# Where the gathered modulation rows and the context blocks stand in TensorE's queue: a two-model transformer stack on one core

## The reference, cut to what matters

```python
for l in range(2):
    ml, mc = silu(c) @ w_ada[l] + b_ada[l], silu(c_ctx) @ w_ada[l] + b_ada[l]   # 9 vectors of 1024 each
    lat += 0.5 * ml[2] * swiglu(rmsnorm(lat) * (1 + ml[1]) + ml[0])             # ffn1, both streams
    cx  += 0.5 * mc[2] * swiglu(rmsnorm(cx)  * (1 + mc[1]) + mc[0])
    lat, cx = mixer(modulated lat, modulated cx)                                # w_in: 1024 -> 3584, then w_out
    lat += 0.5 * ml[8] * swiglu(modulated lat)                                  # ffn2; cx too in layer 0
x = rmsnorm(lat) * g_final
for layer in range(2):                                                          # the second model, 256 tokens
    x += attention(rmsnorm(x) * g) ;  x += relu(rmsnorm(x) * g @ up) ** 2 @ down
```

## Time and profile before

| what | value |
|---|---|
| median of three runs | 2677.27 us |
| the profiled execution's own time | 2683.47 us |
| its span, first to last instruction | 2681.6 us |
| TensorE (PE) busy | 2593.1 us |
| VectorE, ScalarE, GpSimd busy | 1199.1, 1111.2, 885.9 us |
| mean granted TensorE clock | 0.985 of full |

### The profile page before, as it was taken

The page is one execution under the profiler, slowest core; times in us unless marked ns, Lnnn a source line. Parts: engine busy times, 40 slices in busy tenths (PEclk is TensorE's granted clock), DMA queues, the critical chain, the costliest instruction groups (busy, mean ns, idle before and its releaser), DMA issues.

```text
span 2681.6 us, 43982 instructions
## 1 busy us (share of the span) xinstructions
PE 2593.1 (97%) x17121; PEld 2306.9 (86%) x17121; DVE 1199.1 (45%) x1801; ACT 1111.2 (41%) x1544; POOL 885.9 (33%) x1092
## 2 busy tenths in 40 slices
PE   7999999999999999999999999888999999999999
PEld 5787778988888777787777888888999999998999
DVE  4222224227662222252232247654446666556744
ACT  4312333635334222243122247535574555446543
POOL 1222231320013223222232226304554445553554
PEclk9999999999999999999999999999999999999999
DMA  6343632430023333333334333323454434452444
GB/s 251 135 176 141 173 141 109 142 127 1 32 79 149 142 141 142 142 115 130 133 149 158 127 145 138 109 86 143 179 186 153 157 142 179 182 186 105 166 177 153
DMA packets 58527, 376.89 MB, mean 141 GB/s; under 512 B 6223, under 2 KB 12007, under 8 KB 14216
## 3 DMA queue, kind: packets, MB, share of 16 engines
q1 hardware_dynamic: 56988, 371.53, 37.4%
q10 hardware_dynamic: 1388, 3.16, 0.8%
HBM read 370.46 MB, written 3.16 MB: 139 GB/s over the span
## 4 chain that ended last, share of the span: by engine, by line
issue 54%; PE 26%; POOL 17%; DVE 1%; ACT 1%; POOLq 0%; DMA 0%; SPq 0%; DVEq 0%; ACTq 0%
POOL WL L1919 17%; PE PSA L566 8%; PE PSA L567 8%; PE PSA L568 8%; PE PSA L645 1%; ACT WH L1366 0%; POOLq L398 0%; PE PSA L1200 0%; PE PSA L1227 0%; PE PSA L1151 0%; PE PSA L1128 0%; PE PSA L1172 0%; DMA X<-in_x 0%; DMA RAW<-in_weights 0%; POOLq L1917 0%
## 5 line engine op out<-in xcount | busy, mean ns | idle before, releaser
L1919 POOL TENSOR_TENSOR WL<-RAW,WH 128x256 fp32r<-128x256 f32 x1088 | 885.7, 844 | 1783.3 <-ACT WH L1366 1783.3
L1366 ACT ACTIVATE WH<-RAW 128x1024 fp32r<-128x1024 f32 x544 | 545.7, 1050 | 923.8 <-PE PSA L568 879.0
L1942 DVE TENSOR_TENSOR WL<-RAW,WH 128x1024 fp32r<-128x1024 f32 x272 | 340.4, 1252 | 1113.0 <-ACT WH L1366 1112.8
L566 PE MATMUL PSA<-HH,WH 128*128 128x512 f32 (+1 forms) x1664 | 597.7, 359 | 22.1 <-DVE HL L2037 5.2
L567 PE MATMUL PSA<-HL,WH 128*128 128x512 f32 (+1 forms) x1664 | 590.3, 355 | 0.0
L568 PE MATMUL PSA<-HH,WL 128*128 128x512 f32 (+1 forms) x1664 | 589.4, 354 | 0.0
L566 PE MATMUL PSA<-GH,WH 128*128 128x256 f32 (+1 forms) x1664 | 528.1, 317 | 4.8 <-DVE GL L1959 4.8
L567 PE MATMUL PSA<-GL,WH 128*128 128x256 f32 (+1 forms) x1664 | 521.2, 313 | 0.0
L568 PE MATMUL PSA<-GH,WL 128*128 128x256 f32 (+1 forms) x1664 | 521.0, 313 | 0.0
L566 PEld LDWEIGHTS PSA<-HH,WH 128*128 128x128 f32 x1664 | 317.3, 191 | 81.6 <-issue 22.4
L568 PEld LDWEIGHTS PSA<-HH,WL 128*128 128x128 f32 x1664 | 317.4, 191 | 43.8
(11 more groups left out here) (326 smaller groups left out, 2968.8 us busy)
## 6 DMA issues: line engine op xcount, KB each, us to landing
RAW<-in_weights SPq DMA_DIRECT2D x272, 1024.0 KB, 4.9
ADA<-in_w_ada SPq DMA_DIRECT2D x65, 1024.0 KB, 4.9
Zada<-in_w_ada SPq DMA_DIRECT2D x7, 1024.0 KB, 15.6
scratch_bias<-BREL ACTq DMA_DIRECT2D x1, 2048.0 KB
SUMS<-in_c_sums SPq DMA_DIRECT2D x1, 1664.0 KB, 8.2
TB<-scratch_bias SPq DMA_DIRECT2D x1, 1536.0 KB, 12.1
X<-in_x SPq DMA_DIRECT2D x1, 1024.0 KB, 6.0
X<-in_ctx SPq DMA_DIRECT2D x1, 1024.0 KB, 9.0
```

What stands on the lines that cost most here:

```text
L566: pe.matmul(out, a_hi, b_hi, start=start, stop=False)
L1366: act.activation(WH[:, j, 4 * h:4 * h + 4, :], RAW[:, j, 4 * h:4 * h + 4, :], ACT.Copy)\
L1919: ins = pool.tensor_tensor(WL[:, j, kb, :], RAW[:, j, kb, :], WH[:, j, kb, :].bitcast(F32), ALU.subtract)
L1942: dve.tensor_tensor(WL[:, j, 0:4, :], RAW[:, j, 0:4, :], WH[:, j, 0:4, :].bitcast(F32), ALU.subtract)\
```

## The change

In words:

1. **Turns.** `ADAR` goes. In w_in the rows still gather in bank 7; in ffn_up and down phases they gather in half of bank 6. The turn no longer waits there for the modulations to be read (`mods_read`); the finish does. In ffn_up and down phases the turn moves from behind the pair's second slot to behind its first. The finish of the phase before now stands behind the next phase's first turn instead of ahead of it.
2. **Added sums.** `added_sums` for a late norm moves from the end of the down phase to behind the first slot of the next phase.
3. **Context blocks.** `pair_by_stream` works by block: slot 0 on context `kb` 0 to 4, then alternately slot 1 on `kb` 0, 1, 2 and slot 0 on `kb` 5, 6, 7, then the sums of squares, then slot 1 on `kb` 3 to 7, then the latent halves. The wait for the second pair of banks, and with it that for slot 1's low part, moves ahead of slot 0's `kb` 5. In w_in both token blocks are done for each `kb`; which bank holds which token block changes, and ScalarE's read-out with it.
4. **First norm.** Four buffers of 256 columns in place of two for the squares. `first_root(0)` stands one block later.

```diff
-        ADAR = PSA[:, 7, 256:512]
+        def ada_rows_of(ph):
+            return bank(7 if ph["kind"] == "w_in" else 6)[:, 256:512]
             def ada_turn(ph, it):
-                pe.wait_ge(mods_read, n.at(mods_read))
+                if ph["kind"] == "w_in":
+                    pe.wait_ge(mods_read, n.at(mods_read))
                 pe.wait_ge(ada_landed, it * 16 + 16 * (ph["ada"] // 2 - 6))
-                ada_rows(ADAR, ADA, it, it == 0, it == ada_its(ph) - 1)
-            def ada_finish(ph):
+                ada_rows(ada_rows_of(ph), ADA, it, it == 0, it == ada_its(ph) - 1)
+            def ada_finish(ph, gated=0):
                 its = ada_its(ph)
+                pe.wait_ge(mods_read, n.at(mods_read) - gated)
                 pe.wait_ge(rows_copied, ph["ada"] // 2 + its)
                 ada_columns(2 * (ph["ada"] % ADA_HELD), 0, its)
             def ada_behind(ph, it, j):
-                if j == 0 and it == 0 and ph["turns"]:
-                    ada_finish(ph["turns"])
-                if has_ada(ph, it):
-                    if j == (0 if ph["kind"] == "w_in" else 1):
-                        ada_turn(ph, it)
-                    elif ph["kind"] == "w_in" and it == ada_its(ph) - 1:
-                        ada_finish(ph)
+                if j == 0 and has_ada(ph, it):
+                    if it == 0 and ph["turns"]:
+                        pe.wait_ge(rows_copied, ph["ada"] // 2)
+                    ada_turn(ph, it)
+                    if it == 0 and ph["turns"]:
+                        ada_finish(ph["turns"], int(PLAN[PLAN.index(ph) - 1]["kind"] == "gate"))
+                if j == 1 and ph["kind"] == "w_in" and it == ada_its(ph) - 1:
+                    ada_finish(ph)
...
                         if (ph["squares"] or ph["feeds"]) and 2 * it + j:
                             if not adds_squares(ph):
                                 unit_sums(ph, 2 * it + j - 1)
-                            elif 2 * it + j == 3:
-                                added_sums(ph)
                         if begins and j == 0:
                             if ph["late"]["fed_by"].get("by_pair"):
                                 unit_sums(ph["late"]["fed_by"], 2)
+                            else:
+                                added_sums(ph["late"]["fed_by"])
                             unit_sums(ph["late"]["fed_by"], 3)
...
                 def pair_by_stream():
...
+                        for m in range(2):
+                            if kind == "w_in":
+                                tok = slice(P * (2 * s + m), P * (2 * s + m) + P)
+                                mm = three(bank(2 * j + m)[:, t], HH[:, kb, tok], HL[:, kb, tok], WH[:, j, kb, :], WL[:, j, kb, :],
+                                           kb == 0, kb == KB - 1)
...
-                    for j in range(2):
-                        pe.wait_ge(bank_read[j], ph["unit"] + BANK_CREDIT)
-                        half(j, 1)
-                        if j == 0:
-                            part_sums(3, 0)
-                    for j in range(2):
-                        half(j, 0).then_inc(mm_done, 1)
+                    ahead = 5
+                    pe.wait_ge(bank_read[0], ph["unit"] + BANK_CREDIT)
+                    for kb in range(KB):
+                        if kb == ahead:
+                            pe.wait_ge(bank_read[1], ph["unit"] + BANK_CREDIT)
+                        if kb >= ahead:
+                            block(1, 1, kb - ahead)
+                        block(0, 1, kb)
+                    part_sums(3, 0)
+                    for kb in range(KB - ahead, KB):
+                        block(1, 1, kb)
+                    for j in range(2):
+                        for kb in range(KB):
+                            mm = block(j, 0, kb)
+                        mm.then_inc(mm_done, 1)
...
             def first_norm():
...
+                quarters = S2[:].rearrange("p a (b t) -> p (a b) t", b=2)
+                for s in range(2):
+                    for kb in range(KB):
+                        n.take(sq_ready)
+                        pe.matmul(bank(4 - s)[:, 0:NL], ones, quarters[:, kb % 4, :], start=kb == 0, stop=kb == KB - 1)\
+                            .then_inc(sq_used, 1)
...
-                            out = Ztm[:, (which + 1) % 4, per * m:per * m + per, 256 * j:256 * j + 256]
+                            blocks = slice(m, 4, 2) if i < 2 else slice(per * m, per * m + per)
+                            out = Ztm[:, (which + 1) % 4, blocks, 256 * j:256 * j + 256]
...
-                dve.tensor_copy(ROWS[:, 0, :], ADAR).then_inc(rows_copied, its)
+                dve.tensor_copy(ROWS[:, 0, :], ada_rows_of(ph)).then_inc(rows_copied, its)
```

More of the change, by code:

```diff
@@ L783, in pair_by_stream, with block @@
                 def pair_by_stream():
[L785 to L789, removed]
-                            if j == 0:
[L791 to L803, removed]
+                    def block(j, s, kb):
+                        t = streams(512)[s][1]
+                        if s == 1:
+                            slot_half(ph["slot"] + j, kb)
+                        if j == 0:
+                            pe.wait_ge(h_ready, hbase + KB * (1 - s) + kb + 1)
+                        for m in range(2):
[3 more added lines that the diff above has]
+                                           kb == 0, kb == KB - 1)
+                            else:
                                 w = slice(P * m, P * m + P)
@@ L825, in body_of_two_slot_units @@
                             mm.then_inc(mm_done, 1)
-                        if ph["feeds"] and 2 * it + v == 3:
-                            added_sums(ph)
                 def units_by_half():
@@ L848, in units_by_half @@
                             mm.then_inc(mm_done, 1)
-                            if half and u == 3:
-                                added_sums(ph)
                 def units_by_pair():
@@ L1296, in first_norm @@
             def first_norm():
[L1298 to L1303, removed]
+                quarters = S2[:].rearrange("p a (b t) -> p (a b) t", b=2)
[4 more added lines that the diff above has]
+                            .then_inc(sq_used, 1)
+                        if s and kb == 3:
+                            first_rows(0)
+                n.squares += 2 * KB
                 first_rows(1)
@@ L1455, in norm @@
                     act.activation(RSTD[:, 0:1], PR[:, PRM["sel"]:PRM["sel"] + 1], ACT.Sqrt)
[L1456 to L1464, removed]
+                    quarters = S2[:].rearrange("p a (b t) -> p (a b) t", b=2)
+                    for s, t in streams(N):
+                        if s:
+                            act.wait_ge(ctx_landed, 16)
+                        for kb in range(KB):
+                            if s == 0 and kb % 4 == 0:
+                                n.take(x_ready)
+                            if n.squares >= 4:
+                                act.wait_ge(sq_used, n.squares - 3)
+                            act.activation(quarters[:, kb % 4, :], X[:, kb, t], ACT.Square).then_inc(sq_ready, 1)
+                            n.squares += 1
+                            if s and kb == 3:
+                                first_root(0)
                     first_copy(0)
```

## The result

The changed kernel takes 2658.39 us, the median of four runs (2657.78 to 2659.84). The kernel before, run beside it, took 2680.14 us (2676.43 to 2684.7, four runs). The ratio is 0.9908, 95% interval [0.9896, 0.992]: faster by 21.8 us. The profiled execution's span is 2656.0 us where it was 2681.6.

The account below looks back on a forecast made before the run. TensorE, busy 2593.1 of 2681.6 us, was taken as the bound, so only standstills and half clock could move. Terms 1.6 + 8.6 - 1.1 + 7.6 + 0.6 + 3.8 = 21.1 off 2677.3 gave 2656.2 us, range 2649 to 2669 with rivals.

Parts of the forecast that it names:

- A: First norm: four square buffers shorten the first sums, so the first weights start earlier; 1.6 us saved, at most 4.3.
- B: The two w_in behind a norm by stream: latent half done 5.3 us earlier each, less 2 for low clock; 8.6 saved.
- C: The two ffn_up behind a norm by stream: one wait exchanged for another, nothing gained; -1.1 us, between +2 and -5.
- D: Turn behind the first slot: SyncE issues loads a slot sooner, the 4.81 us standstill near 337 us goes; 7.6 saved.
- E: Finish behind the turn: costs nothing, and the one wait for a group goes; 0.6 us saved.
- F: Added sums later: the 1.9 us wait at 2021 us and the half clock behind it go; 3.8 us saved.
- The group is late instead: Under the bias table's DMA the group lands at 329.3 us whenever issued; D = -4.0, time 2668; chance 0.17.
- The standstills stay, low clock after each: Waiting for slot 1's low part lowers the clock at all four norms; B = 3, C = -5, time 2666; chance 0.2.
- Only small change: Both first rivals at once: about 0 to 8 us saved, 2669 to 2677 us; chance 0.08.
- slower: Turns wait on loads that collide with weights, say ten by 3 us; 8 us slower, 2685 us; chance 0.04.

Follow-up runs that it names:

- e2_blocks: The kernel before with only the new order of the context blocks (part 3 of the change); 2673.6 us, ratio 0.996.
- e7_warm4: Changed kernel without interleaving, VectorE's slot 1 low part behind the last context block, ten added matmuls ahead of the first sums, four square buffers; 2647.7 us.
- e1_turns: The kernel before with only the changed turns (part 1: bank 6, behind the pair's first slot, finish behind the next turn); 2675.6 us, ratio 0.9968.
- e9_late5: Changed kernel, interleaving kept, with VectorE's low part for slot 1 moved behind the last context block; 2674.78 us, ratio 0.997.
- e5_ahead8: Changed kernel with the interleaving taken out (ahead = 8 in place of 5: no slot 1 blocks among slot 0's); 2658.98 us, ratio 0.9915.
- e3_first: The kernel before with only the four square buffers in the first norm (part 4); 2680.26 us, ratio 0.9984.
- e4_added: The kernel before with only the added sums moved later (part 2); 2679.66 us, ratio 0.9982.

## Why the prediction was right, step by step

The forecast was 2656.2 us with a range of 2649 to 2669, and 2658.39 was measured; the saving was 21.8 us where the sum gave 21.1. The terms:

| step | predicted | measured in the profiles |
|---|---|---|
| A first norm | 1.6 | 0.6 here; 0.8 alone; 1.4 in the mean of nine |
| B two w_in | 8.6 | 5.24 + 5.09 = 10.3 |
| C two ffn_up | -1.1 | -0.1 and -1.2 (`e2_blocks`) |
| D turn, SyncE's queue | 7.6 | 7.4 (6.7 alone) |
| E group wait | 0.6 | the wait, at 1545.08 us before, is gone: 0.6 |
| F added sums | 3.8 | 3.9 (3.1 alone, by span) |
| not in the sum | 0 | 3.1, the clock behind two unchanged waits; some 1.0 in small differences |

**A** was sized well in the mean and too high for this execution. In the kernel before the squares pass at 0.85 us for the first five sums and at 0.62 from 14.3 us on, so I counted four sums as slow. In the changed kernel's profile the slow pace lasted until 16.8 us, seven sums, and left four buffers little to do. `e7_warm4` shows that this pace is TensorE's own: the same engines, buffers and semaphores pass a sum in 0.42 us when matmuls went before.

**B** is the term that was mis-sized most, by 1.7 us. The mechanism was right: the wait of 1.6 us for L1942 measured 1.42, and the turn stands 12.46 us behind the sums where 12.6 was forecast. The loss of 2 us for a low clock after the wait came at none of the four norms in two kernels. So B was 10.3; the 5.3 for each, the figure without that loss, measured 5.24 and 5.09.

**C** held: no gain, and -1.3 in all. The norms ahead of ffn_up were already on the pattern; a wait was only exchanged.

**D** held in the dates of the group. Issue at 297.3 us (298.4 forecast), landing 19.6 us later at 316.9 (318.1), turn at 319.5 (320.4), no wait. For the weights behind it the transfer time was wrong: issued at 302.8 (303.6 forecast), they took 17.6 us and not 22, and landed at 320.4 where 325.9 was forecast. The error was on the safe side, since the split had to be in time for slot 26 and was. The Trainium skill (DMA: Bandwidth & Descriptors, "Queues, rings and completion order") has an engine drain a whole packet of up to 64 descriptors before it changes queues, which by the prediction's estimate would have let the group land as late as 325 us. No run here shows the packets themselves.

**E and F** held. `ACC` is complete at 1999.3 us, where 1997.43 and 1.85 us of VectorE's last addition end, and is summed at 2003.0.

**The rivals.** *The group is late instead* would have had it land at 329.3 us whenever it is issued. It landed at 316.9; this rival is refuted by the changed kernel and by `e1_turns`. The comparison is a clean one, because ScalarE issues the bias table's transfer at the same time in both kernels (before, then after), and the group stands 16.4 us behind it in the one and 4.1 us in the other:

```profile
293.20 1.30 ACTq L1895 DMA_DIRECT2D scratch_bias<-BREL  x1
293.28 1.30 ACTq L1908 DMA_DIRECT2D scratch_bias<-BREL  x1
```

*The standstills stay, low clock after each* is refuted for a wait of 1.42 us, eight times out of eight, but its mechanism is real. In `e9_late5` the same wait is 3.43 us and the clock is low behind it all four times, which with what stands around it costs 25.5 us. What separated my forecast from that rival was the length of one wait, 1.4 or 3.4 us. *Only small change* and *slower* needed the first two or many late groups; there was none.

**What was luck.** 3.1 us of the ledger come from two waits that are the same in both kernels, with a low clock behind them in one profiled execution and not in the other. The 1.7 us of pace in step F are of the same kind: behind the wait for `ACC`, 1.9 us, the clock fell in three of the four profiles that have it. The forecast was taken off the median of three runs, 2677.27; the kernel before has since shown medians of 2680 to 2685 us. Against 2684.66, its median over the most runs (not beside the changed kernel), the gain is 26 us, and the sum of 21.1 is 5 us short. Why the clock falls behind a given wait in one execution and not in another stays open; no run was aimed at it.

## What to carry to other kernels

Where an engine's queue is in order, ask of each instruction in the middle of a critical chain who needs it soonest. The change moved TensorE's blocks around a low part that VectorE makes in the middle of the context norm's chain, before its user needs it; moving that one instruction behind the chain, without the interleaving, was worth 9.1 us over the changed kernel, while the interleaving alone changed nothing in the total, and the late low part with the interleaving cost 16. A release moved one slot earlier moved its load by a slot here, even under another queue's large transfer, and cost nothing where two slots lay between release and use. Price a removed wait twice, for its length and for the pace behind it: by the working of steps D and F, 4.5 of their 11.4 us were pace. Count the pace in full only for a long wait; behind those of 1.9 to 2.2 us the clock fell in 13 cases of 27.

## What the runs showed of the hardware

- **The clock's row and the pace at the start disagree.** Both windows here have a granted clock of 1.00, the changed kernel first, then `e7_warm4`:

```profile
10.00:17.00 7.00, 6.41 (x16) 5.21 (x17) 1.13 (x1) 3.99 (x11) 0.00 (x0) 1.00 1.03 422
```

```profile
12.00:17.00 5.00, 5.00 (x27) 4.12 (x30) 1.17 (x2) 4.43 (x12) 0.00 (x0) 1.00 1.01 421
```

 The first has 16 records in 6.4 us of work, 2.5 a microsecond, and the second 5.4. At the very start of an execution the distance between instructions tells the pace, and the row doesn't. The Trainium skill (TensorE: Matmul & The Clock Gate, "What's actually happening") says that "the default state is throttled, and activity releases the throttle"; by that, TensorE would start at 1.2 GHz, and the trace agrees in the pace (0.85 us a sum without earlier matmuls, 0.42 with) though not in the row.
- **Length of a wait and the clock behind it.** This counts, in all eleven profiles, the waits of one place or kind behind which the granted clock had a mean under 0.9 in the next 3 us. The low part of slot 1 (L1955 in the changed kernel) at the norms, 1.42 us: 0 of 8. `ACC`, 1.9 us: 3 of 4. The low parts at the norms, 2.11 us: 4 of 12 (at 786.27 and not at 1179.84 us in the kernel before, once in four in `e5_ahead8`). `KE`, 2.2 us: 6 of 11. The low parts ahead of w_in in the kernel before, `e1_turns`, `e3_first` and `e4_added`, 2.46 us: 8 of 8. GpSimd, 2.8 us: 10 of 11. The same low part, 3.43 us in `e9_late5`, and that of the first slot, 3.40 us: 15 of 15. The length of one wait isn't all of it: in the second mixer, where a wait of 1.50 us for `RQ` at 1770.53 us stands in a row of shorter ones, the kernel before has a clock of 0.66 from 1772 to 1784 us.
- **The latent norm is a chain of constant length.** From the sums behind slot 0's context blocks to the turn behind its latent half it is 12.46 to 12.48 us in the changed kernel and in the five built on it, at all four norms, whatever stood ahead.
- **The group's load under the bias table's transfer took as long from either start.** The 1 MB group took 19.7 us when it was issued at 309.6 us and 19.6 us when it was issued at 297.3. That isn't so for every load there: the weights issued next took 22.2 us from 310.6 and 17.6 us from 302.8. The median over all 1 MB weight loads of an execution is 4.9 us before and 4.8 after.
